# Delta rule of a prompt: state products between two key products, one state residual ahead of the second mask, output sum ahead of a substitution piece

## What is computed

```python
lower = jnp.where(strict, jnp.einsum('...ik,...jk->...ij', kb, kc) * dmask, 0.0)
sol = lax.linalg.triangular_solve(jnp.eye(C) + lower, rhs, left_side=True, lower=True)
u, w = sol[..., :dv], sol[..., dv:]
intra = jnp.einsum('...ik,...jk->...ij', qc, kc) * dmask
def step(S, xs):
    v_new = u_i - jnp.einsum('bhck,bhkv->bhcv', w_i, S)
    o = jnp.einsum('bhck,bhkv->bhcv', q_i * jnp.exp(G_i)[..., None], S) + jnp.einsum('bhij,bhjv->bhiv', a_i, v_new)
    S = S * jnp.exp(g_last)[..., None, None] + jnp.einsum(
        'bhck,bhcv->bhkv', k_i * jnp.exp(g_last[..., None] - G_i)[..., None], v_new)
    return S, o
```

## Time and profile before

| quantity | value |
|---|---|
| median of three executions | 2648.53 us |
| the profiled execution | 2650.03 us |
| its span | 2648.3 us |
| TensorE busy | 2411.5 us (91%) |
| VectorE busy | 1619.1 us (61%) |
| prompt's delta rule in it | about 1692 to 2011 us |

### The profile page before, as it was taken

How to read it: one execution, slowest core, us unless ns; L and a number is a source line. 1 busy time by engine, 2 the same in 40 slices (tenths; PEclk the granted TensorE clock), 3 DMA queues, 4 the chain that set the end, 5 groups by cost and what they waited for, 6 DMA issues and landing times. The chain is left out here.

```text
span 2648.3 us, 44338 instructions
## 1 busy us (share of the span) xinstructions
PE 2411.5 (91%) x16770; PEld 2129.1 (80%) x16770; DVE 1619.1 (61%) x3710; ACT 1108.6 (42%) x2268; POOL 235.5 (9%) x432
## 2 busy tenths in 40 slices
PE   5999999999999999999995997678877489999996
PEld 2777788888999999999995885577776189999774
DVE  6766765553637676665552665588774467765654
ACT  4544444444214444444443664245443233331443
POOL 0000000001111111000000001111110001111000
PEclk7999999999999999999998998688886699999998
DMA  6223233234322323233225438565524645656442
GB/s 244 96 112 112 96 111 113 96 111 168 112 82 94 109 94 106 97 109 99 99 83 211 175 126 302 130 172 148 136 72 138 219 132 180 186 151 206 140 138 73
DMA packets 249434, 356.26 MB, mean 135 GB/s; under 512 B 54819, under 2 KB 187555, under 8 KB 243974
## 3 DMA queue, kind: packets, MB, share of 16 engines
q1 hardware_dynamic: 189538, 223.51, 27.7%
q0 software_dynamic: 33264, 116.90, 11.5%
q10 hardware_dynamic: 26420, 13.01, 1.8%
HBM read 241.23 MB, written 112.11 MB: 133 GB/s over the span
## 5 line engine op out<-in xcount | busy, mean ns | idle before, releaser
L295 PE MATMUL ps_f<-m_lo,w_hi 128*128 128x272 f32 (+1 forms) x2436 | 789.6, 324 | 13.5 <-DVE m_lo L605 6.8
L295 PE MATMUL ps_f<-m_hi,w_hi 128*128 128x272 f32 (+1 forms) x2436 | 793.3, 326 | 0.0
L295 PE MATMUL ps_f<-m_hi,w_lo 128*128 128x272 f32 (+1 forms) x2436 | 784.8, 322 | 0.0
L295 PEld LDWEIGHTS ps_f<-m_lo,w_hi 128*128 128x128 f32 x2436 | 458.9, 188 | 68.4 <-issue 32.9
L295 PEld LDWEIGHTS ps_f<-m_hi,w_lo 128*128 128x128 f32 x2436 | 459.6, 189 | 36.7
L295 PEld LDWEIGHTS ps_f<-m_hi,w_hi 128*128 128x128 f32 x2436 | 458.7, 188 | 33.8
L669 DVE TENSOR_TENSOR stage<-partial,ps_f 128x512 f32<-128x512 f32 (+2 forms) x348 | 171.3, 506 | 318.3 <-PE ps_f L295 306.8
L420 ACT ACTIVATE partial<-ps_f 128x272 f32<-128x272 f32 (+1 forms) x348 | 160.9, 462 | 392.7 <-PE ps_f L295 391.0
L382 ACT ACTIVATE w_hi<-w_raw 128x512 fp32r<-128x512 f32 x348 | 213.1, 625 | 204.2 <-PE ps_f L295 128.1
L576 DVE TENSOR_TENSOR w_lo<-w_raw,w_hi 128x512 fp32r<-128x512 f32 x348 | 239.0, 688 | 85.0 <-ACT w_hi L382 81.5
L65 PE MATMUL ps_fm<-u_lo,w_tail_hi 128*128 128x256 f32 (+1 forms) x768 | 221.7, 289 | 12.8 <-DVE u_lo L2907 8.2
(11 more groups left out here) (415 smaller groups left out, 3936.3 us busy)
## 6 DMA issues: line engine op xcount, KB each, us to landing
w_raw<-in_w_feat SPq DMA_DIRECT2D x58, 1024.0 KB, 5.9
gates<-scratch_g_d SPq DMA_DIRECT2D x56, 256.0 KB, 3.2
z_f<-scratch_z_d ACTq DMA_DIRECT2D x16, 768.0 KB, 5.1
scratch_conv_d<-conv POOLq DMA_DIRECT2D x18, 544.0 KB, 3.0
scratch_conv_d<-conv POOLq DMA_DIRECT2D x18, 512.0 KB, 2.9
kc<-in_k_cache SPq DMA_DIRECT2D x8, 1152.0 KB, 14.1
vc<-in_v_cache POOLq DMA_DIRECT2D x8, 1152.0 KB, 9.9
scratch_g_d<-stage POOLq DMA_DIRECT2D x16, 544.0 KB, 4.5
```

Of the source, the lines that this page charges most:

```text
L295: last = pe.matmul(out[:, 0:n], l[:, cols], r, start=start and k == 0 and nth == 0, stop=k == KH - 1 and nth == 2, skip_group_check=not start)
```

## The change

No function changes its body; only the order of calls in TensorE's and VectorE's streams changes. TensorE issues `of_state(c + 1)` between `grams(a)` and `grams(a + 1)`. VectorE issues `result(c)` ahead of piece 6 of the substitution (it was between the two masks), and `residual(c + 1)` ahead of `mask(a + 1)`.

```diff
@@ TensorE
                 if later(it + 2):
-                    grams(a), grams(a + 1)
+                    grams(a)
                 if has(it):
                     of_state(c + 1)
+                if later(it + 2):
+                    grams(a + 1)
                 if has(it + 1):
                     turn_keys(b + 1)
@@ VectorE
                 if later(it + 1):
-                    solve(it + 1, 5), solve(it + 1, 6), solve(it + 1, 7)
+                    solve(it + 1, 5)
+                if has(it):
+                    result(c)
+                if later(it + 1):
+                    solve(it + 1, 6), solve(it + 1, 7)
                 if later(it + 2):
                     mask(a)
                 if has(it):
-                    result(c)
+                    residual(c + 1)
                 if later(it + 2):
                     mask(a + 1)
-                if has(it):
-                    residual(c + 1)
                 if has(it + 1):
                     turn_diag(b), turn_diag(b + 1)
```

## The result

The changed kernel took 2664.39 us in the median of six executions (2657.56 to 2668.86); the kernel before, in the same comparison, 2648.86 us. The ratio is 1.0047, with a 95% interval from 1.0034 to 1.0061: about 12 us (9 to 16) slower. The two medians lie 15.5 us apart, more than the ratio says, and the runs do not tell why; so 12 to 16 us have to be explained. By the ratio the forecast's base of 2648.53 us becomes 2661.0 us. The forecast was 2656.0 with a range up to 2661.5: the direction was right, the size too small, and the result stands at the range's upper edge (by the difference of the medians it would be 2664.1, outside it). The profiled execution took 2665.34 us, a span of 2663.6 us, which is 15.3 us above the span before.

The account below looks back on a forecast made before the run. The stage was taken to be bound by a transfer chain ending in sub_u, which the first pivot awaits. Terms 6.5 - 3.0 + 4 = +7.5 us gave 2656.0 us against the median, range 2649.5 to 2661.5.

Parts of the forecast that it names:

- What bounds the stage: Each iteration's first pivot (S) waits for sub_u, behind a chain of stores and loads after the last pivot (X).
- The output sum, 0.93 us times seven: Output sum moved between first and last pivot delays all behind it by 0.93 us in iterations 0 to 6: plus 6.5.
- the wait moves with it: In iteration 6 the sub_w store and VectorE's 3.71 us wait for TT come 0.93 us later, so cost 0.93.
- The residual waits, minus 3.0 us: VectorE's waits for TensorE's state products, 1.3, 1.2 and 0.5 us in iterations 1 to 3, vanish: minus 3.0.
- The residual's move at no cost: Residual ahead of second masks: last pivot (X) to second masks' end (M) stays about 5.2 us; cost about 0.
- TensorE's new order: State products use TensorE's 3.52 us wait ahead of the second chunk's products; up to 0.4 us exposed, taken as 0.
- its cover: State products fit before the second chunk's key products are needed, about 5 us after X; cover just enough.
- The transfers, plus 4 us of a possible 8.2: Earlier decay loads disturb sub_u in iterations 0 to 3; bounds 0 and 8.2 us, middle taken: plus 4.
- near 13: Sign of disturbance: second masks' end to first pivot in iterations 0 to 3, 11.8 us on the mean if undisturbed.
- From X to the first `sub_u` load: SyncE's second store was to leave as long after the last pivot as before, 5.2 to 5.3 us; cost about 0.

Follow-up runs that it names:

- experiments 1 and 2: 1: SyncE's loads behind sub_u held until the first pivot, on changed kernel 1.0020, on kernel before 0.9993; 2: gates ahead of second state, on kernel before, 1.0028.
- experiments 9 and 10: 9: kernel before, first chunk's store ahead of TT loads, 0.9991; 10: changed kernel, that plus sub_u all on SyncE and iteration 6's sum at its old place, 1.0007.
- Experiment 4: Kernel before with the output sum ahead of piece 6 in iteration 6 alone; ratio 1.0010 to the kernel before.
- early_gates: Kernel before with VectorE's two gates ahead of the second state, so decay loads leave sooner; ratio 1.0028 to the kernel before.
- loads_held: Changed kernel with all SyncE loads behind sub_u waiting for the first pivot of the next substitution; ratio 1.0020 to the kernel before.
- experiment 8: Changed kernel with the residual back behind the second masks, output sum and TensorE's order as changed; ratio 1.0040 to the kernel before.
- experiment 7: Changed kernel with TensorE's order as before, state products behind both chunks' key products; ratio 1.0049 to the kernel before.
- held_last_old: Changed kernel with SyncE's next loads held until the first pivot and iteration 6's output sum at its old place; ratio 0.9997 to the kernel before.
- one_queue: Changed kernel with all eight sub_u parts of pairs 1 to 7 issued by SyncE, none by GpSimd; ratio 1.0005 to the kernel before.
- experiment 6: All sub_u parts of pairs 1 to 7 issued by SyncE: on the changed kernel 1.0005, on the kernel before 0.9995.
- tensor_undone: Changed kernel with TensorE's state products again behind both chunks' key products; ratio 1.0049 to the kernel before.

## Why the prediction was right, and what it sized wrongly

*What bounds the stage* was right: S waited for `sub_u` in every iteration, and an edit that only moves loads in time (experiments 1 and 2) moved the kernel by 7 us either way. It was incomplete: TensorE's chain lies close behind, as experiments 9 and 10 show.

*The output sum, 0.93 us times seven.* In iterations 0 to 5 right within 0.2 us: S to X became 21.95 us in iterations 1, 2, 4 and 5, where it had been 21.2 without the residual waits. In iteration 6 it was mis-sized: from iteration 5's first pivot to the end of the stage 62.1 us passed instead of 59.0, about 3.2 us and not 0.9. Experiment 4 tells this part by itself. The step that failed is "the wait moves with it": I did not look at what TensorE would do with its time there, and at where its lower clock would then fall.

*The residual waits, minus 3.0 us.* All gone: in iterations 0 to 5 no first residual of the changed kernel waits for TensorE. By itself that proves little, since in `early_gates` a later first pivot removed them too, with TensorE's order untouched. `loads_held` is the better witness: its pivots come as early as before, and S to X is still 22.0 to 22.4 us. The term was somewhat larger than 3.0: S to X of iterations 1 to 5 lay 3.9 us above five times the undisturbed 21.15 before.

*The residual's move at no cost, and TensorE's new order.* Supported: X to M stayed at 5.2 us, and experiment 8 changed nothing. That TensorE's part is worth its cover showed only as a wait, not as time (experiment 7).

*The transfers, plus 4 us of a possible 8.2.* This is the term that was mis-sized. The load legs grew by 8.4 us over iterations 0 to 3, and holding the loads back gave 7 us, with iteration 4's part in it. I took the middle, and the sum came out at the upper bound taken from iteration 4 (1.8 us there, 1.9 here, where I had forecast 2.2). That it met 8.2 so closely is in part luck. By the measure of the forecast itself, M to S of iterations 0 to 3, the growth was 10.2 us and the mean 14.3 us, not "near 13"; two of the four stretches lie above iteration 4's 13.84 (17.19 and 14.46), two below (13.04 and 12.62). The mechanism was right and its size was not; nothing in the rows spoke for half of it.

*The rest.* From X to the first `sub_u` load 64.8 us passed in six iterations, before 61.0. In three other runs with the changed order on both engines (`loads_held`, `held_last_old`, `one_queue`) it was 62.2 to 62.5 us. So 1.2 to 1.5 us of it come with the order, about 1 us of that in iteration 5 of each, for a reason that I did not find; the rest is scatter of the one execution, whose 15.3 us stand above the 12 of the ratio. The forecast had put this at nothing.

With the terms at their measured size the sum would be 4.8 (six sums at 0.8) + 3.2 (iteration 6) - 3.9 + 8.4 + 1.3 = about 14 us. The profiled execution can be added up as well: the stage grew by 1.2 us in S to X, 3.9 in X to the first load, 8.3 in the legs and 3.2 behind iteration 5's first pivot, 16.6 in all, and the rest of the span was some 1.2 us shorter. The three terms that were too low (transfers, iteration 6, X to the first load) all erred to the same side, and that the result lies within the range at all, by the ratio, is close to luck.

The Trainium skill ("DMA: Bandwidth & Descriptors", section on queues, rings and completion order) states that DMA engines serve queues in turn and each ring in order; that speaks for a disturbance of GpSimd's half. The traces agree: the part that ends the wait is GpSimd's fourth (65 of 66 legs), and SyncE's own packets ended 4.0, 6.1, 4.4 and 4.8 us after the first load in the changed kernel's iterations 0 to 3, before it 4.5, 4.6, 4.0 and 6.7. That keeping all parts in one queue protects them by order was not shown (experiment 6).

## What to carry to other kernels

When a small, scattered transfer ends a cycle, look at what its neighbours in time are: an edit on a compute engine that lets the next bulk load start 3 us sooner can cost more than all the compute it moves. Look which part of it lands last, and who issues that part. Where the nearest row has a cause that the change brings closer, a reason is needed for taking less than its full value. And before filling an engine's idle time, ask what that idle time held back: here the late gates kept the queue clear, and the late output sum kept TensorE's gap and its lower clock in a place where nothing waited for it.

## What was not expected of the hardware

The disturbance is steep: decays issued 1.8 to 1.9 us behind the first `sub_u` load lengthened the leg by 2.1 to 2.4 us on the mean of four iterations (0.9 to 3.9 us in single ones); at 2.7 to 3.2 us it was 0.5 on the mean, which is within the scatter of the undisturbed runs. The part that suffered was the last of four that GpSimd issued, and not those of the queue in which the bulk loads stood. Moving twelve products of TensorE 4 us ahead in iteration 6 left it idle for 4.97 us ahead of the inverse, and the granted clock over the 8 us from the transposes on was 0.60 instead of 1.00. Two 384 KB stores issued together held the `sub_u` loads back for 4.6 to 5.6 us from the first one's start (kernel before); with the second issued 3 to 4.7 us later (`tensor_undone`) the loads left 2.2 to 2.6 us after its issue had ended in iterations 0 to 4, and 4.3 us in iteration 5.
